# Two transformer blocks on one core: the chunk inverse kept in PSUM, paired products in the chunk steps, modulation work in another order

## What is computed

```
t_mat = a_strict + eye(64)
value      = triangular_solve(t_mat, v_beta, unit_diagonal=True)
k_cumdecay = triangular_solve(t_mat, k_beta * exp(decay))
def step(S, inp):                      # once per chunk
    qd, kc, val, att, kt, cd = inp
    v_new = val - kc @ S
    o = qd @ S + att @ v_new
    S = S * cd + kt.T @ v_new
    return S, o
```

```
mod = silu(c) @ w_ada + b_ada          # 1024 x 6144
sh1, sc1, g1, sh2, sc2, g2 = split(mod, 6)
h  = rmsnorm(x, norm_mix) * (1 + sc1) + sh1
x  = x + g1 * (merged @ w_out)
h2 = rmsnorm(x, norm_ffn) * (1 + sc2) + sh2
x  = x + g2 * moe(h2)
```

## Time and profile before

| | us |
|---|---|
| median of three runs | 1146.23 (1145.27 to 1148.15) |
| the profiled execution | 1137.32 |
| its span in the trace | 1135.5 |
| TensorE busy | 1106.6 (97%) |
| VectorE, ScalarE, GpSimd busy | 603.9 (53%), 501.5 (44%), 151.2 (13%) |
| mean granted TensorE clock of the core | 0.998 |

### The profile page before, as it was taken

One profiled execution on the slowest core, in us unless ns is written; L12 is line 12 of the kernel. 1 busy time (PEld: TensorE's weight loads), 2 busy tenths in 40 slices (PEclk: granted clock), 3 DMA queues, 4 the chain that ended last, 5 costly groups with the idle time before them and its releaser, 6 DMA issues.

```text
span 1135.5 us, 18601 instructions
## 1 busy us (share of the span) xinstructions
PE 1106.6 (97%) x7625; PEld 843.2 (74%) x7625; DVE 603.9 (53%) x925; ACT 501.5 (44%) x827; POOL 151.2 (13%) x111
## 2 busy tenths in 40 slices
PE   8999799999999999999999999999999999999996
PEld 7987678999878888778888876666666666666663
DVE  5988676879956784785755652222222222222223
ACT  6665654654433746645556252222222222222223
POOL 1339960422000040400000000000000000000000
...
GB/s 314 280 215 77 297 93 201 161 263 257 183 306 204 243 176 223 211 162 154 174 157 329 209 288 423 421 426 423 423 425 420 425 422 421 425 424 421 426 421 175
DMA packets 82701, 332.05 MB, mean 292 GB/s; under 512 B 4555, under 2 KB 6926, under 8 KB 66110
## 3 DMA queue, kind: packets, MB, share of 16 engines
...
q10 hardware_dynamic: 298, 0.11, 0.1%
...
HBM read 329.83 MB, written 1.05 MB: 291 GB/s over the span
## 4 chain that ended last, share of the span: by engine, by line
PE 80%; DVE 8%; DMA 7%; issue 2%; ACT 2%; SPq 1%; DVEq 0%; ACTq 0%
PE bank L1113 18%; PE bank L451 12%; PE bank L453 12%; PE bank L452 12%; PE bank L1132 9%; PE bank L1103 5%; DMA ring<-in_w_exp_down 3%; DVE ring_r L1844 2%; DMA ring<-in_w_in 2%; DVE arena L1924 2%; PE bank L1160 1%; PE bank L1161 1%; DMA ring<-in_w_ff 1%; DMA ring<-in_w_ada 1%; PE bank L1120 1%
## 5 line engine op out<-in xcount | busy, mean ns | idle before, releaser
L1844 DVE TENSOR_TENSOR ring_r<-ring,arena_r 128x2048 fp32r<-128x2048 f32 x93 | 217.9, 2355 | 118.5 <-ACT arena_r L1333 116.9
L1333 ACT ACTIVATE arena_r<-ring 128x2048 fp32r<-128x2048 f32 x93 | 177.4, 1918 | 170.1 <-PE bank L453 71.7
L453 PE MATMUL bank<-arena_r,actT_r 128*128 128x512 f32 x384 | 150.5, 392 | 0.0
L451 PE MATMUL bank<-arena_r,tok_r 128*128 128x512 f32 x352 | 140.8, 400 | 1.7 <-DVE con L2331 1.7
L452 PE MATMUL bank<-ring_r,tok_r 128*128 128x512 f32 x352 | 138.2, 393 | 0.0
L2688 POOL TENSOR_TENSOR ring<-ring 128x512 f32<-128x512 f32 x63 | 102.5, 1652 | 253.7 <-ACT ring L1424 251.9
L2503 DVE TENSOR_TENSOR arena<-bank,arena 64x512 f32<-64x512 f32 x62 | 42.7, 688 | 175.3 <-PE bank L1132 174.6
L451 PE MATMUL bank<-tok_r,arena_r 128*128 128x256 f32 x352 | 99.5, 283 | 1.8 <-DVE actT_r L1861 1.2
L453 PE MATMUL bank<-tok_r,ring_r 128*128 128x256 f32 x352 | 98.3, 279 | 0.0
L452 PE MATMUL bank<-actT_r,arena_r 128*128 128x256 f32 x352 | 98.2, 279 | 0.0
L2489 DVE TENSOR_TENSOR arena<-bank,arena 128x256 f32<-128x256 f32 x32 | 13.6, 425 | 151.3 <-ACT arena L1763 93.9
...
## 6 DMA issues: line engine op xcount, KB each, us to landing
...
```

The costliest lines, as they stand in the source:

```text
L451: mm(o, l[0], r[0], start=start, stop=False)
L453: return mm(o, l[1], r[0], start=False, stop=stop)
L1333: A(hi, w, ACT.Copy).then_inc(S["w_high"], 1)
L1844: TT(half(i, ringR)[0], w, hi.bitcast(fp32), ALU.subtract).then_inc(S["w_rest"], 1)
```

## The change

- D and its transpose are kept for all levels in two banks, one for each t, as 512 columns [D | transposed D]. TensorE adds each level's corrections onto them, for D and its transpose in one go (`D{l}{t}`); the rotation skips these banks (`held`). ScalarE copies them to `DIT` (`inverse_copies`). `corrected` is gone.
- The gate product is made in two halves, in levels 0 and 1; the attention's transposes stay in level 2 and the scores in 3 and 4. No modulation chunk stands in the levels.
- kc alternates between the two 64-row halves of two banks. It lies interleaved with q in `KQ`, so that one product of 128 rows gives kc S and q S in vp{n}. The product att v_new of two chunks, alternating in the same way, is added onto those rows (do0 with do1, do2 with do3).
- The state is first scaled (`decayed`, one operation for four heads), and sn{n} is added later. Where VectorE read two semaphores for handing on (`a_max`, `s_new`), the read counts of the banks do.
- Chunks 1 and 0 are both added by GpSimd, from the read of dg1 on; 1 is scaled by ScalarE and 0 by GpSimd. ada(1) stands behind kc, ada(0) behind the chunk steps. Chunk 2 is made by VectorE ahead of `o_rest(1)` and transposed behind the output product; 3 stands in ff1, and 4 and 5 are made by VectorE in steps 9 and 13 of the second block. sc1 is formed behind ff2's low parts.

```diff
...
+        ET, RR, AT, MT = [x[:, 0:8 * C] for x in (ar(15360, 1024), QD, kbT, qT)]
+        YY = DQ[:, 8 * C:16 * C]
+        DIT = [x[:, 0:8 * C] for x in (DQ, DK)]
+        VAL, VN = KB, ar(15360, 1024)
+        KQ = [QD, qdT]
...
-        ADA_BY_POOL = (0, 4)
-        ADA_BY_DVE = (7, 8, 9)
-        DVE_MOD = {4: 8, 10: 9}
...
+        ADA_BY_POOL = (1, 0, 3, 6, 10, 11)
+        ADA_BY_DVE = (2, 7, 8, 9, 4, 5)
+        DVE_FF2 = {3: 8, 10: 9}
+        DVE_STEP = {9: 4, 13: 5}
...
-        ADA_BEHIND = {("win", 2): (0,), ("win", 6): (1, 2, 3, 4), ("ff1", 2): (5,), ("ff1", 5): (6,), ("ff2", 0): (7,),
-                      ("ff2", 3): (8,), ("ff2", 6): (9,), ("win2", 2): (10,), ("win2", 6): (11,)}
+        ADA_BEHIND = {("win", 6): (1, 0), ("wout", 1): (2,), ("ff1", 2): (3,), ("ff1", 5): (6,), ("ff2", 0): (7,),
+                      ("ff2", 3): (8,), ("ff2", 6): (9,), ("win2", 2): (10,), ("win2", 6): (11,), ("win2", 10): (4,),
+                      ("wret", 0): (5,)}
...
+            while turns[0] % 8 in held:
+                turns[0] += 1
...
+                    pe.wait_ge(S["pool_step"], 4 + 3 * ADA_BY_POOL.index(c) + (c != 1))
...
+                for h in range(DH):
+                    for r in (0, C):
+                        i = mm(bk[r:r + C, (4 + h) * C:(5 + h) * C], K("identC")[r:r + C, :], turned_inverse(4 * t + h, r),
+                               start=False, stop=True, skip_group_check=True)
                 end(i, f"D0{t}")
+                held.append(where[f"D0{t}"][0])
...
-                    split_product("win", 6, "dg")
-                elif l == 1:
-                    ada(0)
+                if l < 2:
+                    dg_half(l)
                 elif l == 2:
-                    ada(1)
                     att_turn()
                 elif l == 3:
                     att_scores((0, 1))
-                else:
-                    ada(2)
+                elif l == 4:
                     att_scores((2, 3))
...
-                    wait_read(pe, f"D0{t}" if l == 0 else f"Dn{l - 1}{t}")
-                    product(f"Y{l}", AT, DI, t)
+                    wait_read(pe, f"D{l}{t}")
+                    chunk_products(f"Y{l}", t, lambda bk, h, r: bk[r:r + C, h * C:(h + 1) * C], within(AT), inverse)
                     if t == 0:
                         fill(l)
                 for t in range(T):
                     wait_read(pe, f"Y{l}{t}")
...
-                    if not last:
-                        product(f"Dn{l}", DT, YY, t)
-                    product(f"Dt{l}", YY, DT, t)
+                    bk = begin_at(f"D{l + 1}{t}", held[t])
+                    for turned in (1,) if last else (0, 1):
+                        for h in range(DH):
+                            for r in (0, C):
+                                two = (turned_inverse(4 * t + h, r), within(YY)(4 * t + h, r))
+                                i = mm(bk[r:r + C, (4 * turned + h) * C:(4 * turned + h + 1) * C], two[turned],
+                                       two[1 - turned], start=False, stop=True, skip_group_check=True)
+                    end(i, f"D{l + 1}{t}")
+            held.clear()
             for t in range(T):
-                wait_read(pe, f"Dt{len(LEVELS) - 1}{t}")
+                wait_read(pe, f"D{len(LEVELS)}{t}")
                 wait_read(pe, f"ct2{t}")
-                chunk_products("val", t, lambda bk, h, r: bk[r:r + C, h * P:(h + 1) * P], within(DT), block_rows(DV))
...
+                chunk_products("val", t, lambda bk, h, r: bk[r:r + C, h * P:(h + 1) * P], turned_inverse, block_rows(DV))
+                two = [(r, begin(f"kc{t}_{r}")) for r in (0, C)]
+                for h in range(DH):
+                    for r, bk in two:
+                        i = mm(bk[:, h * C:(h + 1) * C], block_rows(KBE)(4 * t + h, r), turned_inverse(4 * t + h, r),
                                start=True, stop=True)
...
-            ada(3)
+                        if h == DH - 1:
+                            end(i, f"kc{t}_{r}")
+            ada(1)
...
-                    pe.wait_ge(S["s_new"], n)
+                    wait_read(pe, f"sn{n - 1}")
                     bk = begin(f"vp{n}")
                     for h in range(DH):
-                        o = (4 * t + h) * P
-                        i = mm(bk[r:r + C, h * P:(h + 1) * P], KC[:, o + r:o + r + C], old[:, h * P:(h + 1) * P],
-                               start=True, stop=True)
+                        i = mm(bk[:, h * P:(h + 1) * P], KQ[t][:, 256 * h + 2 * r:256 * h + 2 * r + P],
+                               old[:, h * P:(h + 1) * P], start=(h == 0), stop=True, skip_group_check=True)
                     end(i, f"vp{n}")
                     if n == 1:
                         prob_turn(range(4, 8))
+                    elif n == 2:
+                        end(att_values(begin("ao0"), 0, range(8)), "ao0")
                     else:
-                        att_values(n - 2)
-                        if n == 3:
-                            o_turn(0)
-                pe.wait_ge(S["vn_new"], n + 1)
+                        att_values(ao1, 1, range(4, 6))
+                    wait_read(pe, f"vp{n}")
+                else:
+                    pe.wait_ge(S["vn_new"], 1)
...
                 if n == 0:
                     prob_turn(range(4))
-            ada(4)
+                elif n == 2:
+                    ao1 = begin("ao1")
+                    att_values(ao1, 1, range(4))
+                else:
+                    two = [(0, begin("do0") if n == 1 else begin_at(f"do{n - 1}", where[f"vp{n - 1}"][0])),
+                           (C, begin_at(f"do{n}", where[f"vp{n}"][0]))]
+                    for h in range(DH):
+                        for q, bk in two:
+                            o = (4 * t + h) * P
+                            i = mm(bk[C - q:P - q, h * P:(h + 1) * P], MT[q:q + C, (4 * t + h) * C:(4 * t + h + 1) * C],
+                                   VN[q:q + C, o:o + P], start=(n == 1 and q == 0 and h == 0), stop=True,
+                                   skip_group_check=True)
+                            if h == DH - 1:
+                                end(i, f"do{n - 1 + q // C}")
+                    if n == 3:
+                        o_turn(0)
+                        end(att_values(ao1, 1, range(6, 8)), "ao1")
+            ada(0)
...
+            ada(2)
...
+            inverse_copies(3)
+            att_exps((0,))
+            inverse_copies(4)
+            att_exps((1, 2, 3))
+            inverse_copies(5)
+            att_exps((4,))
...
+                    done(copy(v3(KQ[t], DH)[:, :, 3 * r:3 * r + C], v3(bk[:, 0:256], DH)), f"kc{t}_{r}")
+                att_exps((5,) if t == 0 else (6, 7))
...
-                    TT(VN[rows, o], VAL[rows, o], bk[rows, :], ALU.subtract).then_inc(S["vn_new"], 1)
...
+                    done(TT(VN[rows, o], VAL[rows, o], bk[rows, :], ALU.subtract), f"vp{n}")
 
             def new_state(n):
...
+                    bk = wait_full(dve, f"sn{n}")
+                    done(TT(new, new, bk[:, :], ALU.add), f"sn{n}")
+            def decayed(n):
+                o = 8 * (n % 2) + 4 * (n // 2)
+                wait_read(dve, f"sn{n - 1}")
+                tt(v3(states[n % 2], DH), v3(states[(n - 1) % 2], DH), bc(ecd[:, o:o + DH], P), ALU.mult)
...
             new_values(0)
-            mod_cols(3)
             new_state(0)
-            dve.wait_ge(S["a_exp"], AH)
-            step(V.reciprocal(a_rd, a_sum))
             prob_copies((1, 3))
             new_values(1)
+            decayed(1)
+            mod_cols(1)
+            new_state(1)
             prob_copies((5, 7))
-            new_state(1)
+            dve.wait_ge(S["a_exp"], AH)
             wait_read(dve, "val1")
+            new_values(2)
+            step(V.reciprocal(a_rd, a_sum))
+            decayed(2)
...
+            mod_cols(0)
+            mod_sums(2)
             o_rest(1)
-            mod_cols(4)
...
+                if s in DVE_STEP:
+                    mod_sums(DVE_STEP[s])
...
+            wait_read(pool, "dg1")
+            ada(1)
+            ada(0)
+            wait_full(pool, "val1")
...
```

247 lines of the change are left out of this document (108 added, 139 removed).

## The result

| | before | after |
|---|---|---|
| median, us | 1146.12 (1145.27 to 1148.15, 4 runs) | 1135.51 (1134.43 to 1136.43, 4 runs) |
| profiled execution, us | 1137.32 | 1134.83 |
| span in the trace, us | 1135.5 | 1133.0 |

The two profiled executions, however, differ by 2.5 us only (spans), and the sum of the prediction gives 3.05 us for them. So there are two questions: whether the sum is right term by term, and where the other 8 us come from.

A forecast was written before the change was run, and what follows sets the result against it. Expert weights pace the tail, which moves with the TensorE work before it: waits in the levels, small products in the chunk steps. 3.75 - 0.55 - 1.25 + 1.1 = 3.05 us off 1146.23 gave 1143.2 us, range 1138.5 to 1147.0.

The forecast's parts named there:

- the last line of the sum: Whole execution: the median stays 8.9 us above the profiled execution, so 1146.23 - 3.05 = 1143.2 us.
- Levels: Levels of the chunk inverse: waits 5.9, transposes 1.8, D0 -1.15; 6.4 us taken, val0 at 130.0 instead of 136.4.
- Chunk steps: Small products from val0 to vp3: 2.2 us gained, less 0.3 for handoffs; vp3 ends at 151.75 us.
- the paired pace: Chunk steps, instructions alternating the two 64-row halves: 65 to 70 ns each taken, bounds 68 and 180 ns.
- the wait for bank 0: Chunk steps: head 5's transpose waits until VectorE has reduced mod1 and freed the bank; 1.9 us on TensorE.
- Output product: VectorE's queue finishes o_rest(1) at 176.25, TensorE idles 4.4 us before mo01; of 8.3 us gained, 3.75 are left.
- The terms for chunks 2, 4, 5 and 8: After the output product: chunk 2's transpose -0.55, late chunks 4 and 5 -1.25, chunk 8's wait removed +1.1 us.
- Rival C: Before mo01: clock falls in idle time, first 12 products slower, 0 to 2.8 us; gain about 1, 1145.2; chance 0.08.
- Rival A: Output product gives back less, vp3 2 to 4 us earlier; gain 5 to 7, 1137.5 to 1141.2; chance 0.20.
- B: Chunk steps: more small waits, or state scaling at 1.6 us twice; gain 0 to 1.5, 1144.7 to 1146.2; chance 0.13.
- D: Chunk steps: halves don't run side by side, 180 ns per paired instruction; 4 us slower than now, 1150.2; chance 0.09.
- E: GpSimd's modulation additions and products late: mod0 at 164, mo01 at 177.2 us; gain 2.1; chance 0.05.

The follow-up runs named there:

- the old steps with the three moves: Changed kernel with old chunk steps, mod_cols(1) before new_state(0), chunk 2's sums behind the second add_x, third add_x before the low part: 1132.48 us, ratio 0.9913.
- a_sums_late: Changed kernel with mod_cols(0) and mod_sums(2) on VectorE behind the second add_x instead of ahead of o_rest(1): median 1133.85 us, ratio 0.9920 to the kernel before.
- r_before: The kernel before, unchanged, run again: median 1141.92 us, 5 of 10 executions at 1137.0 to 1138.5 and 5 at 1145.3 to 1150.1.
- p_before2: The kernel before, unchanged, profiled once more to meet a long execution: it took 1148.69 us (span 1146.9).

## Why the prediction was wrong

**The step that failed is the last line of the sum,** "the median of the runs shown is 8.9 us above it; I take the same difference off it". I treated the distance between the profiled execution and the median as a constant of the kernel. It is a state of the clock: executions of before at about 1146 us have a mean granted clock of 0.990 to 0.991 instead of 0.998, which is 8 to 9 us more lost at the lower level than in the profiled one, and the long one that was seen loses more than half of its 11.4 us in the chunk steps, which this change rebuilds. In the changed kernel's four executions the offset was not 8.9 us but 0.7 (median 1135.51, profiled 1134.83). Three runs within 3 us of each other and a profile 9 us below them allowed the reading as two groups, and I took only that of an offset.

How much of the 8 us each part of the change takes away is not settled, and part of it is the draw of the first comparison. The changed kernel has 3 of 15 executions in a second group, and that group is 5 us above the first instead of 9; with the old steps on the new levels it was 5 of 12, some 14 us above. That speaks for the new steps. But the old steps with the three moves do as well (2 of 12), so the old steps alone don't decide it either.

**The sum itself against the profile.** Levels: foreseen a gain of 6.4 us at val0, measured about 7.7 (from 136.4 to 128.70). The waits were right (0.63 and 1.01 us where I had 0.75 and 1.4). The term that was mis-sized is D0 with its 32 more instructions: 1.15 us in my sum, 0.76 measured (1.92 us from 93.89 to 95.81, against 1.16 from 94.47 to 95.63). TensorE also came to D0 0.6 us earlier, by small differences ahead of the levels that the sum doesn't have. Chunk steps: foreseen 1.9, measured 1.6 up to the end of vp3; the paired pace (68 and 69 ns) and the wait for bank 0 (2.27, foreseen 1.9) were both there, and ahead of vp3 came 0.52 us for new_state(2). That operation stands behind the scaling of the state, which took 0.96 and 1.79 us, where I took 0.7 twice and named 1.6 as the upper end. In a_sums_late the second scaling started at 148.15, behind GpSimd's last addition (136.99 + 9.29), and took 0.69 us; here it started at 144.88, and the additions ran until 146.12 (136.81 + 9.31):

```profile
148.15 0.69 DVE L1888 TENSOR_TENSOR arena<-arena,small 128x512 f32<-128x512 f32 x1
```

```profile
136.81 9.31 POOL L2731 TENSOR_TENSOR ring<-ring 128x512 f32<-128x512 f32 x7
```

So the same instruction takes up to 2.6 times as long while GpSimd adds. The page "GPSIMD Engine Reference" of the Trainium skill, section "1. Specifications", states this contention, without a size. The trace agrees in part: the windows of the two operations show GpSimd busy in both, yet one took 0.96 us and the other 1.79, and what makes that difference is open:

```profile
137.67:138.63 0.96, 0.00 (x0) 0.00 (x0) 0.96 (x1) 0.09 (x1) 0.96 (x2) 1.00 1.05 410
144.88:146.67 1.79, 1.79 (x17) 1.72 (x17) 1.79 (x1) 1.79 (x2) 1.50 (x2) 1.00 0.00 0
```

Output product: the queue on VectorE was right row by row; mo01 0.9 us earlier than foreseen, since all of it hangs on vp3. The rest: 2.7 us of gain at the end of mo01, 2.6 at 194 us and 2.5 at the first experts' product. The terms for chunks 2, 4, 5 and 8, -0.7 us in my sum, cost 0.2. Part of that is mod2's transpose, 0.35 us on TensorE instead of 0.55; the wait for chunk 8 went, as written.

That the sum came within 0.6 us of the 2.5 measured is partly luck: 0.9 us more at mo01 and 0.5 us less for the rest stand against 2.0 us lost to the clock, which the sum put at nothing.

**Rival C came in.** The clock fell with the 4.79 us of idle time, for 7 us, and took 2 us (ten products at 0.43 instead of 0.236). I gave that 0.08 and its size 0 to 2.8; in the sum it is what brings 4.7 us at mo01 down to 2.7. I argued from the profile before, in which the clock stayed up behind a wait of 2.83 us; r_before and p_before2 show it falling behind that very wait. Rival A (a smaller give-back) is the one on the side of the measured time, but 1135.5 lies below its 1137.5 to 1141.2, and it isn't the mechanism: the give-back was as foreseen (4.6 us: vp3 came 9.3 us earlier, mo01 4.7). Its two statements don't agree either, since a gain of 7 us is 1139.2, and 1137.5 is one of 8.7. Of B, the scaling came near its upper end once, not twice, and its time did not occur; D and E did not occur.
